# Order and waits in the odd layer of a decoder trunk: sigmoids, gate halves, decay constants and the last transposed tile

## The chip, the cores and the metric

The kernel runs on one core of one Trainium2 chip. The core has five engines with a queue each: TensorE (PE, matmuls), VectorE (DVE), ScalarE (ACT), GpSimd (POOL) and SyncE (SP, which only starts transfers here). An engine does its queue in order; between engines only semaphores set the order. The metric is the device time of one execution in microseconds.

## The reference, cut to what matters

Two residual layers over a sequence of 1024 tokens of width 1024, in float32. The first (even) layer is sparse attention beside gated linear attention; the change does not touch what it computes. The second (odd) is a Griffin recurrent block:

```python
h = rmsnorm(x, pre_norm[1])
xr, g = jnp.split(h @ odd_w_in, [1024], axis=-1)     # 1024 x 2048 weights
xr = causal_dwconv(xr, conv_w, conv_b)               # width 4
r = sigmoid(blockwise(xr, w_a) + b_a)                # 4 blocks of 256 x 256
i = sigmoid(blockwise(xr, w_x) + b_x)
a = exp(-8 * r * softplus(-lam))
u = sqrt(-expm1(2 * log_a)) * (i * xr)
hs = recurrence(a, u)                                # h_t = a_t h_(t-1) + u_t
mix = (hs * silu(g)) @ odd_w_out
x = x + rmsnorm(mix, post_norm[1])
```

## The kernel before

The order on each engine is written out by hand, engine by engine; there is no scheduler. A float32 product is made of three fp32r matmuls: each operand is split into a high part (ACT copies it to fp32r, names ending in H) and a low part (DVE or POOL subtracts, names ending in L), and PE adds high x high, high x low and low x high (three, L1583; its matmuls are L1588 to L1590). One matmul has 128 x 128 weights and 512 columns.

**Even output projection and norms (from about 675 us in the trace).** PE makes one tile of 128 tokens at a time (out_tile, 48 matmuls) and between tiles transposes the normalised tile before it into PSUM (turn_h1, L1894, 8 transposes from hn1). ACT copies the transposed tile to h1H (L1040), DVE subtracts to h1L (L1472) and adds to h1l_done. PE's next transposes wait for that semaphore, because they write the same banks. In the loop over tiles DVE does for tile t: post-norm, residual, pre-norm (L1463), and then the split of tile t-1. At t = 4 it calls odd_decay() (L1338 to L1352), 24 operations on 128 x 8 elements that make the constants of the decay; ACT needs them only before the odd layer's weights.

**Odd input projection.** 16 column chunks of weights, each in two halves of 512 tokens (odd_chunk(i), 24 matmuls, banks 0, 1, 6 and 7 in turn). Half 0 of the tokens needs tiles 0 to 3 only, so the first two chunks run before the last tile (7) is transposed; the third needs all tiles.

**The four recurrent blocks n = 0 to 3,** each of 2 x 128 channels (halves j = 0, 1). PE computes the gates (block_gates(n)): per j two groups g = 0, 1 of 12 matmuls into banks 2-3 and 4-5. A group waits, through gate_sig, until ACT's sigmoid (L1079) has emptied that bank pair. ACT writes the sigmoids to t_r and t_i, one buffer per j, shared by all blocks. Then ACT makes the decay (t_a) and a tanh, DVE the ratio, ACT the square root, and DVE multiplies (L1516) and scans (L1517, the recurrence, function recur), and multiplies the result with silu_g (L1521, function gated, which adds to y_done). silu_g comes from PSUM: ACT takes its sigmoid (silu_of, L1070), DVE multiplies it with the bank (silu_half, L1511, adds to silu_g_done), which frees the bank. sigmoids(n) in ACT's queue waits for both gated products of block n-1.

**Odd output projection.** For k = 0 to 7 (the 128-channel slices of y) PE adds to four token tiles at a time (final_part(t, k), 6 matmuls; banks 2, 4, 0, 6 and their neighbours), then tiles 4 to 7 one by one. It needs, per k, the weights w2oH / w2oL (ACT L756, POOL L606) and the split of y (split_y on ACT, low_y on DVE, L1525). Tiles 2 and 3 use banks 0-1 and 6-7, which hold the last block's silu input until silu_half has run.

Of the kernel before, what the change touches and what calls it, by code (L numbers as in the profile page):

```python
# [19 lines left out]
ALU = mybir.AluOpType  # L20
# [6 lines left out]
KD = D // P  # L27
# [10 lines left out]
LRU_BLOCKS = 4  # L38
# [43 lines left out]
def build(nc, x, rel_bias, pre_norm, post_norm, even_w_in, even_gate_w2, gate_b2, even_w_out,  # L82
# [13 lines left out]
    def sem(name):  # L96
        return ctx.enter_context(nc.semaphore(name))
# [8 lines left out]
    y = at("y", [P, KD, T], F32, R0)  # L106
# [245 lines left out]
    gw_in, gw_hi, gw_lo, gw_used = sem("gw_in"), sem("gw_hi"), sem("gw_lo"), sem("gw_used")  # L352
    xr_ready, conv_done, xch_done, xcl_done = sem("xr_ready"), sem("conv_done"), sem("xch_done"), sem("xcl_done")
    odd_full, xr_pad, sgg_done, silu_g_done = sem("odd_full"), sem("xr_pad"), sem("sgg_done"), sem("silu_g_done")
    input_gated = sem("input_gated")
    gate_full, gate_sig, decay_done, tanh_done, ratio_done, mult_done, y_done = (
        sem(n) for n in ("gate_full", "gate_sig", "decay_done", "tanh_done", "ratio_done", "mult_done", "y_done"))
    x2_in, o2_out = [sem("x2_in0"), sem("x2_in1")], [sem("o2_out0"), sem("o2_out1")]
# [384 lines left out]
    def _(act):  # L743
        def high(c):

            act.wait_ge(raw_in[c % 2], 16 * (c // 2 + 1))
            if C_WOE <= c < C_ODD or c >= C_WOO:
                k = c - (C_WOE if c < C_ODD else C_WOO)
                if c < C_ODD:
                    act.wait_ge(proj_full, len(PRODUCTS))  # L750
                    act.activation(woH[:, k, :], raw_row[:, c % 2, :], ACT.Copy).then_inc(w_hi, 1)
                else:
                    act.wait_ge(gate_full, 4 * LRU_BLOCKS)
                    if k >= 2:
                        act.wait_ge(odd_full, len(ODD_HALVES) - (2 if k == 2 else 0))
                    act.activation(w2oH[k][:, :], raw_row[:, c % 2, :], ACT.Copy).then_inc(w_hi, 1)  # L756
                return
            if c >= C_ODD:
                i = c - C_ODD
                if i == 2:  # L760
                    act.wait_ge(mix_full, NT)
                if i >= 3:
                    act.wait_ge(odd_full, ODD_HALVES.index((i - 3, 1)) + 1)
                act.activation(w_slot_H[i % 3][:, :, :], raw[:, c % 2, :, :], ACT.Copy).then_inc(w_hi, 1)  # L764
                return
            if c >= C_AV:
                act.wait_ge(proj_full, last_product(before_in_slot(c)) + 1)
            act.activation(wH[:, dst_slot(c), :, :], raw[:, c % 2, :, :], ACT.Copy).then_inc(w_hi, 1)  # L768
# [301 lines left out]
                act.activation(silu_g[:, j, hf * HALF:(hf + 1) * HALF], ps[:, ODD_BANK[i % 4], :], ACT.Sigmoid).then_inc(sgg_done, 1)  # L1070

        def sigmoids(n):
            if n:
                act.wait_ge(y_done, 2 * n)
            for j in range(2):
                for g, dst, bias in ((0, t_r, bias_a), (1, t_i, bias_x)):
                    act.wait_ge(gate_full, 4 * n + 2 * j + g + 1)
                    b = S_BANK[g]
                    act.activation(dst[:, j, :].rearrange("p (b w) -> p b w", b=2), ps[:, b:b + 2, :], ACT.Sigmoid,  # L1079
                                   bias=bias[:, 2 * n + j:2 * n + j + 1]).then_inc(gate_sig, 1)  # L1080
# [13 lines left out]
        def split_y(k):  # L1094
            if k < 2:
                act.wait_ge(conv_done, 2 * LRU_BLOCKS)
            elif k >= 6:
                act.wait_ge(input_gated, 2 * LRU_BLOCKS)
            act.wait_ge(y_done, k + 1)
            act.activation(ysH[k][:, :], y[:, k, :], ACT.Copy).then_inc(ys_hi, 1)  # L1100
# [40 lines left out]
        split_y(5)  # L1141
        silu_of(n, 1)
        high(C_WOO + 3)
        split_y(6)
        high(C_WOO + 4)
        split_y(7)
        for k in range(5, KD):
            high(C_WOO + k)

        for t in range(NT):  # L1150
# [6 lines left out]
    def _(dve):  # L1157
        steps = Tally(dve_step)

        def own(ins):  # L1160

            steps(ins)
            dve.wait_ge(dve_step, steps.n)
# [44 lines left out]
        n = 0  # L1208
# [247 lines left out]
        for t in range(NT + 1):  # L1456
            if t < NT:
                after(t, S_BANK[t % 2], wpost, post_rms, xt1, tmp1, x1_in, post_done, x1_ready)
                dve.wait_ge(rms1_ready, t + 1)
                own(dve.reciprocal(rstd[:, t:t + 1], rms[:, t:t + 1]))  # L1460
                if t >= 2:
                    dve.wait_ge(h1_turned, t - 1)
                dve.scalar_tensor_tensor(hn1[:, t % 2, :], xt1[:, t % 2, :], rstd[:, t:t + 1], wpre1[:, :],  # L1463
                                         ALU.mult, ALU.mult).then_inc(h1_ready, 1)
                if t == 4:
                    odd_decay()
            if t:
                u = t - 1
                dve.wait_ge(h1h_done, u + 1)
                toks = slice(u * P, (u + 1) * P)  # L1470
                for i in range(2):
                    ins = dve.tensor_tensor(h1L[i][:, :, toks], ps[:, 6 + i, :].rearrange("p (k n) -> p k n", n=P),  # L1472
                                            h1H[:, 4 * i:4 * i + 4, toks].bitcast(F32), ALU.subtract)
                ins.then_inc(h1l_done, 1)

        dve.wait_ge(mix_full, NT)
        dve.memset(xr[:, :, 0:3], 0.0).then_inc(xr_pad, 1)
# [35 lines left out]
        def recur(n, j):  # L1513
            dve.wait_ge(mult_done, 2 * n + j + 1)
            dve.wait_ge(input_gated, 2 * n + j + 1)
            own(dve.tensor_tensor(t_i[:, j, :], t_i[:, j, :], t_r[:, j, :], ALU.mult))  # L1516
            own(dve.tensor_tensor_scan(y[:, 2 * n + j, :], t_a[:, j, :], t_i[:, j, :], 0.0, ALU.mult, ALU.add))  # L1517

        def gated(n, j):
            dve.wait_ge(silu_g_done, 4 * n + 2 * j + 2)  # L1520
# [35 lines left out]
            silu_half(n, 0, hf)  # L1556
        low_y(3)
        recur(n, 0)
        gated(n, 0)
        recur(n, 1)  # L1560
        for k in (4, 5):
            low_y(k)
        for hf in range(2):
            silu_half(n, 1, hf)
        gated(n, 1)
        for k in (6, 7):
            low_y(k)
        dve.wait_ge(row_in, 48)

# [7 lines left out]
    def _(pe):  # L1577
# [323 lines left out]
        with rounds(pe, (NT - 2) // 2) as i:  # L1901
            for s in range(2):
                out_tile(2 * i + s + 2, s, *even, post_done, mix_full)
                turn_h1(2 * i + s + 1, 1 - s)
        def odd_chunk(i):
            c, hf = ODD_HALVES[i]
            if hf == 0:
                pe.wait_ge(w_lo, C_ODD + c + 1)
            if i >= 4:
                conv, gates = evictions(i - 4)  # L1910
                if ODD_SEQ[ODD_HALVES[i - 4][0]][1] < 2:
                    pe.wait_ge(xr_ready, conv)
                else:
                    pe.wait_ge(silu_g_done, gates)
            weights_first(ODD_BANK[i % 4], (w_slot_H[c % 3], w_slot_L[c % 3]), hf,
                          xs=(lambda k: h1H[:, k, :], lambda k: h1L[k // 4][:, k % 4, :])).then_inc(odd_full, 1)

        def block_gates(n):
            pe.wait_ge(xcl_done, 2 * n + 2)
# [11 lines left out]
                    last.then_inc(gate_full, 1)  # L1931

        odd_chunk(0)
        odd_chunk(1)
        turn_h1(NT - 1, 1)
        pe.wait_ge(post_done, NT)
        pe.wait_ge(h1h_done, NT)
        pe.wait_ge(h1l_done, NT)
# [16 lines left out]
        for k in range(KD):  # L1955
            pe.wait_ge(w_lo, C_WOO + k + 1)
            pe.wait_ge(ys_lo, k + 1)
            for t in range(4):
                if k == 0 and t >= 2:
                    pe.wait_ge(silu_g_done, 4 * LRU_BLOCKS - 2 * (3 - t))  # L1960
                last = final_part(t, k)
                if k == KD - 1:
                    last.then_inc(mix2_full, 1)
        for t in range(4, NT):
# [58 lines left out]
```

## Time and profile before

| | before |
|---|---|
| median of 3 runs | 1117.87 us (1117.31 to 1119.39) |
| the profiled execution | 1114.39 us |
| its span, first to last instruction | 1112.6 us |
| its mean granted TensorE clock | 0.961 |
| PE busy | 1011.4 us (91%) |
| DVE busy | 689.8 us (62%) |
| ACT busy | 458.0 us (41%) |
| POOL busy | 268.1 us (24%) |

How to read the rows below. A row of a timeline gives the start in us, the duration in us, engine, line, operation, output<-inputs, shape, the number of merged instructions (x), and in brackets the idle time of the engine just before and who ended it. A row of the list of waits reads: engine, what waited, its line, what it waited for and its line, then us in total, times, longest. A row on one tile's instructions gives the count, then min/median/max ns and first and last start in us. A row of busy time by stretch gives the stretch, its length, the busy us of PE, weight load, DVE, ACT and POOL (instructions), the granted clock (1.00 is 2.4 GHz, 0.50 is 1.2 GHz), DMA share and GB/s. Ends of matmuls are modelled.

### The profile page before, as it was taken

To read this page: it belongs to the slowest core of one execution; us is meant where nothing else is said; L and a number is where in the kernel's file an instruction comes from. 1 tells how busy PE (TensorE), PEld (TensorE's weight loads), DVE (VectorE), ACT (ScalarE), POOL (GpSimd) and SP (SyncE) were. 2 spreads that over 40 slices of the span, in tenths; PEclk is the share of its full clock that TensorE was granted. 3 is DMA by queue.
4 is the path that set the end of the run, shared out by engine and by line. 5 is a ranking of instruction groups with operands and counts; after the bars stand their busy time and mean duration, and the time that the engine had idled before them with its cause. 6 is when DMAs were issued, how large, how long until landed. Compare 5 with 4: busy or idle time off the path is not lost.

```text
span 1112.6 us, 14632 instructions
## 1 busy us (share of the span) xinstructions
PE 1011.4 (91%) x5642; PEld 815.4 (73%) x5642; DVE 689.8 (62%) x1220; ACT 458.0 (41%) x780; POOL 268.1 (24%) x199
## 2 busy tenths in 40 slices
PE   4996889989999999789999778989999999895997
PEld 3885679968877776557777566878788888684885
DVE  5314679997779597874554462574539393967042
ACT  6323552253422323335555563433246363573031
POOL 2210212102332322313131564120313122124000
PEclk8998999989999999899999898999999999997999
DMA  7251102101112223101010434322211121112052
GB/s 242 63 71 38 39 1 77 39 1 38 57 56 87 76 67 114 40 25 43 16 53 24 156 106 154 111 75 76 81 52 57 38 57 39 38 38 92 22 189 75
DMA packets 71738, 75.81 MB, mean 68 GB/s; under 512 B 5064, under 2 KB 58360, under 8 KB 71672
## 3 DMA queue, kind: packets, MB, share of 16 engines
q1 hardware_dynamic: 70400, 73.30, 21.1%
q10 hardware_dynamic: 1272, 1.62, 1.3%
q8 instruction: 43, 0.70, 0.3%
q14 instruction: 23, 0.19, 0.1%
HBM read 58.13 MB, written 16.25 MB: 67 GB/s over the span
## 4 chain that ended last, share of the span: by engine, by line
PE 76%; DVE 13%; ACT 5%; issue 4%; POOL 1%; DMA 1%; DVEq 0%; SPq 0%; POOLq 0%; ACTq 0%
PE ps L1588 21%; PE ps L1590 20%; PE ps L1589 20%; PE ps L1833 2%; PE ps L1817 2%; PE ps L1676 2%; PE ps L1768 1%; DVE prob L1370 1%; PE ps L1678 1%; PE ps L1765 1%; PE ps L1677 1%; ACT relu L861 1%; DVE ysL L1525 1%; PE ps L1736 1%; DVE y L1517 1%
## 5 line engine op out<-in xcount | busy, mean ns | idle before, releaser
L1588 PE MATMUL ps<-hH,wH 128*128 128x512 f32 x384 | 159.1, 414 | 15.5 <-DVE qkL L1358 10.0
L1228 DVE TENSOR_SCALAR_CACHE_REDUCE junk<-score,cand 128x384 bf16<-128x384 f32 (+2 forms) x192 | 169.7, 942 | 1.3
L1590 PE MATMUL ps<-hH,wL 128*128 128x512 f32 x384 | 152.7, 398 | 0.0
L1589 PE MATMUL ps<-hL,wH 128*128 128x512 f32 x384 | 152.3, 397 | 0.0
L612 POOL TENSOR_TENSOR wL<-raw,wH 128x1024 fp32r<-128x1024 f32 x32 | 77.1, 2413 | 157.3 <-ACT wH L768 157.3
L1588 PE MATMUL ps<-h1H,w_slot_H 128*128 128x512 f32 x256 | 100.4, 392 | 2.5 <-DVE h1L L1472 2.5
L1590 PE MATMUL ps<-h1H,w_slot_L 128*128 128x512 f32 x256 | 100.3, 392 | 0.0
L1589 PE MATMUL ps<-h1L,w_slot_H 128*128 128x512 f32 x256 | 100.2, 391 | 0.0
L1588 PEld LDWEIGHTS ps<-hH,wH 128*128 128x128 f32 x384 | 73.6, 192 | 35.3 <-issue 21.3
L1590 PEld LDWEIGHTS ps<-hH,wL 128*128 128x128 f32 x384 | 73.6, 192 | 16.2
L1589 PEld LDWEIGHTS ps<-hL,wH 128*128 128x128 f32 x384 | 73.9, 192 | 13.3
L1588 PE MATMUL ps<-wH,hH 128*128 128x256 f32 x256 | 74.7, 292 | 0.0
L1589 PE MATMUL ps<-wL,hH 128*128 128x256 f32 x256 | 73.6, 288 | 0.0
L1590 PE MATMUL ps<-wH,hL 128*128 128x256 f32 x256 | 73.6, 287 | 0.0
L609 POOL TENSOR_TENSOR w_slot_L<-raw,w_slot_H 128x1024 fp32r<-128x1024 f32 x16 | 41.3, 2582 | 132.2 <-ACT w_slot_H L764 132.2
L973 ACT ACTIVATE prob<-prob,small 128x128 f32<-128x128 f32 (+7 forms) x64 | 49.7, 777 | 46.5 <-DVE small L1376 46.4
L1446 DVE RECIPROCAL small<-small 128x1 f32<-128x1 f32 x16 | 2.6, 161 | 102.7 <-ACT small L781 102.7
L984 ACT ACTIVATE pT<-ps 128x512 f32<-128x512 f32 (+3 forms) x96 | 41.9, 487 | 57.7 <-PE ps L1817 57.5
L1370 DVE CUSTOM_DVE_ANT_0 prob<-ps,score 128x384 f32<-128x384 f32 (+5 forms) x48 | 42.7, 890 | 31.4 <-POOL score L692 24.9
L1588 PE MATMUL ps<-w2oH,ysH 128*128 128x512 f32 x128 | 50.8, 397 | 12.1 <-DVE silu_g L1511 11.7
L1588 PEld LDWEIGHTS ps<-h1H,w_slot_H 128*128 128x128 f32 x256 | 48.5, 189 | 12.8 <-issue 2.7
L1589 PEld LDWEIGHTS ps<-h1L,w_slot_H 128*128 128x128 f32 x256 | 48.5, 189 | 10.1
(242 smaller groups left out, 2266.7 us busy)
## 6 DMA issues: line engine op xcount, KB each, us to landing
raw<-in_even_w_in SPq DMA_DIRECT2D x32, 512.0 KB, 4.0
xt<-in_x SPq DMA_DIRECT2D x16, 512.0 KB, 5.6
raw<-in_odd_w_in SPq DMA_DIRECT2D x16, 512.0 KB, 3.9
gate_d<-gst SPq DMA_DIRECT2D x16, 256.0 KB, 2.2
raw_row<-in_even_w_out SPq DMA_DIRECT2D x8, 512.0 KB, 3.4
x_d<-xt SPq DMA_DIRECT2D x8, 512.0 KB, 2.6
raw_row<-in_odd_w_out SPq DMA_DIRECT2D x8, 512.0 KB, 3.2
xt<-x_d SPq DMA_DIRECT2D x8, 512.0 KB, 4.7
```

Of the source, the lines that this page charges most:

```text
L609: pool.tensor_tensor(w_slot_L[s][:, :, :], raw[:, c % 2, :, :], w_slot_H[s][:, :, :].bitcast(F32), ALU.subtract).then_inc(w_lo, 1)
L612: pool.tensor_tensor(wL[:, s, :, :], raw[:, c % 2, :, :], wH[:, s, :, :].bitcast(F32), ALU.subtract).then_inc(w_lo, 1)
L973: act.activation(prob[:, i, 0:w], prob[:, i, 0:w], ACT.Exp, bias=nmx[:, c:c + 1], accum_out=lsum[:, c:c + 1]).then_inc(exp_done[e], 1)
L984: act.activation(pT[:, e, 0:m * P], ps[:, TURN_BANK[e], 0:m * P], ACT.Copy).then_inc(turn_out, 1)
L1228: return steps(dve.tensor_scalar(junk1[:, j % 3, 0:(qb + 1) * P], score_of(qb), threshold, None, op, ALU.add, accum_out=dst[:, j:j + 1]))
L1370: dve.tensor_tensor_reduce(out=prob[:, i, 0:w].rearrange("p (b w) -> p b w", b=banks), in0=ps[:, b:b + banks, 0:wb], in1=mask_of(qb).rearr ...
L1588: pe.matmul(dst, lH, rH, start=k == 0, stop=False)
L1589: pe.matmul(dst, lH, rL, start=False, stop=False)
L1590: return pe.matmul(dst, lL, rH, start=False, stop=k == nk - 1)
L1676: yield pe.matmul(ps[:, b + i, 0:wb], qh, kh[:, cols], start=True, stop=False)
L1817: last = pe.transpose(ps[:, TURN_BANK[e], i * P:(i + 1) * P], prob[:, buffer_of(n, e), (first + i) * P:(first + i + 1) * P], ident[:, :])
L1833: both = [pe.matmul(ps[e * A_DIM:(e + 1) * A_DIM, 7, 0:P], v[:, kb, (2 * p + e) * A_DIM:(2 * p + e + 1) * A_DIM], pT[:, e, i * P:(i + 1) * ...
```

## The change

Four edits.

1. sigmoids(n) on ACT waits, per half j, for a new semaphore recurred that recur(n-1, j) adds to after its scan, instead of once for both gated products of block n-1.
2. In the last block DVE does the two silu halves of j = 1 directly behind recur(3, 0), and all of low_y(4) to low_y(7) behind the second gated product. On ACT the weights of k = 4 and k = 5 each move one place ahead. On PE tile 3 of the output projection skips k = 0 and makes it up at k = 1, and so does its wait for the silu halves.
3. odd_decay() is called behind the split of tile 3 instead of ahead of it.
4. PE transposes tile 7 between the two halves of the sum over k of odd chunk 1.

```diff
         def sigmoids(n):
-            if n:
-                act.wait_ge(y_done, 2 * n)
             for j in range(2):
+                if n:
+                    act.wait_ge(recurred, 2 * (n - 1) + j + 1)
                 for g, dst, bias in ((0, t_r, bias_a), (1, t_i, bias_x)):
...
         high(C_WOO + 3)
+        high(C_WOO + 4)
         split_y(6)
-        high(C_WOO + 4)
+        high(C_WOO + 5)
         split_y(7)
-        for k in range(5, KD):
+        for k in range(6, KD):
             high(C_WOO + k)
...
                                          ALU.mult, ALU.mult).then_inc(h1_ready, 1)
-                if t == 4:
-                    odd_decay()
             if t:
                 u = t - 1
...
                 ins.then_inc(h1l_done, 1)
+            if t == 4:
+                odd_decay()
...
-            own(dve.tensor_tensor_scan(y[:, 2 * n + j, :], t_a[:, j, :], t_i[:, j, :], 0.0, ALU.mult, ALU.add))
+            dve.tensor_tensor_scan(y[:, 2 * n + j, :], t_a[:, j, :], t_i[:, j, :], 0.0, ALU.mult, ALU.add).then_inc(recurred, 1)
+            dve.wait_ge(recurred, 2 * n + j + 1)
...
         recur(n, 0)
+        for hf in range(2):
+            silu_half(n, 1, hf)
         gated(n, 0)
         recur(n, 1)
-        for k in (4, 5):
-            low_y(k)
-        for hf in range(2):
-            silu_half(n, 1, hf)
         gated(n, 1)
-        for k in (6, 7):
+        for k in range(4, KD):
             low_y(k)
...
         odd_chunk(0)
-        odd_chunk(1)
+        odd_chunk(1, range(KD // 2))
         turn_h1(NT - 1, 1)
+        odd_chunk(1, range(KD // 2, KD))
...
             for t in range(4):
-                if k == 0 and t >= 2:
-                    pe.wait_ge(silu_g_done, 4 * LRU_BLOCKS - 2 * (3 - t))
-                last = final_part(t, k)
+                if (k, t) == (0, 2):
+                    pe.wait_ge(silu_g_done, 4 * LRU_BLOCKS - 2)
+                if (k, t) == (1, 3):
+                    pe.wait_ge(silu_g_done, 4 * LRU_BLOCKS)
+                    final_part(t, 0)
+                if (k, t) != (0, 3):
+                    last = final_part(t, k)
```

How this moves the instructions. DVE, last block, from the product ahead of the first scan to the last split of y, before (line numbers of the kernel before):

```order
L1516 TENSOR_TENSOR t_i<-t_i,t_r 128x1024
L1517 SCALAR_TENSOR_TENSOR y<-t_a,t_i 128x1024
L1521 TENSOR_TENSOR y<-y,silu_g 128x1024
L1516 TENSOR_TENSOR t_i<-t_i,t_r 128x1024
L1517 SCALAR_TENSOR_TENSOR y<-t_a,t_i 128x1024
L1525 TENSOR_TENSOR ysL_159<-y,ysH_151 128x1024
L1525 TENSOR_TENSOR ysL_160<-y,ysH_152 128x1024
L1511 TENSOR_TENSOR silu_g<-ps,silu_g 128x512 x2
L1521 TENSOR_TENSOR y<-y,silu_g 128x1024
L1525 TENSOR_TENSOR ysL_161<-y,ysH_153 128x1024
L1525 TENSOR_TENSOR ysL_162<-y,ysH_154 128x1024
```

And the same stretch now (the line numbers are one or two higher):

```order
L1517 TENSOR_TENSOR t_i<-t_i,t_r 128x1024
L1518 SCALAR_TENSOR_TENSOR y<-t_a,t_i 128x1024
L1512 TENSOR_TENSOR silu_g<-ps,silu_g 128x512 x2
L1523 TENSOR_TENSOR y<-y,silu_g 128x1024
L1517 TENSOR_TENSOR t_i<-t_i,t_r 128x1024
L1518 SCALAR_TENSOR_TENSOR y<-t_a,t_i 128x1024
L1523 TENSOR_TENSOR y<-y,silu_g 128x1024
L1527 TENSOR_TENSOR ysL_159<-y,ysH_151 128x1024
L1527 TENSOR_TENSOR ysL_160<-y,ysH_152 128x1024
L1527 TENSOR_TENSOR ysL_161<-y,ysH_153 128x1024
L1527 TENSOR_TENSOR ysL_162<-y,ysH_154 128x1024
```

The silu halves of j = 1 went from behind two splits of y, in eighth place, to third place, behind the first scan; the four splits now stand together at the end.

PE, start of the output projection (ysH_147 and ysL_155 are k = 0, ysH_148 and ysL_156 k = 1; w2oH_163 and w2oH_164 their weights), the six matmuls of tile 3 that arrive behind tile 2 of k = 1, with what they wait for:

```order
 L1590 MATMUL ps<-w2oH_164,ysL_156 128x512
+L1588 MATMUL ps<-w2oH_163,ysH_147 128x512 [waits silu_g_done]
+L1589 MATMUL ps<-w2oL_171,ysH_147 128x512
+L1590 MATMUL ps<-w2oH_163,ysL_155 128x512
+L1588 MATMUL ps<-w2oH_163,ysH_147 128x512
+L1589 MATMUL ps<-w2oL_171,ysH_147 128x512
+L1590 MATMUL ps<-w2oH_163,ysL_155 128x512
 L1588 MATMUL ps<-w2oH_164,ysH_148 128x512
```

Before, the same six stood 18 matmuls further ahead, directly behind tile 2 of k = 0, with the same wait.

PE, odd chunk 1, where the transposes of tile 7 (from hn_126) now stand:

```order
 L1589 MATMUL ps<-h1L_131,w_slot_H_134 128x512
 L1590 MATMUL ps<-h1H,w_slot_L_137 128x512
+L1894 MATMUL ps<-ident,hn_126 128x128 x8
 L1588 MATMUL ps<-h1H,w_slot_H_134 128x512
 L1589 MATMUL ps<-h1L_132,w_slot_H_134 128x512
```

They stood 12 matmuls later, between the end of chunk 1 and the start of chunk 2.

## Rows read from the trace of the kernel before

**Rows 1.** The page, part 4: the chain that ended last, by engine.

```profile
PE 76%; DVE 13%; ACT 5%; issue 4%; POOL 1%; DMA 1%; DVEq 0%; SPq 0%; POOLq 0%; ACTq 0%
```

**Rows 2.** The list of waits, engine PE, 690 to 1113 us.

```profile
PE ps L1588 <- DVE silu_g L1511: 11.7, 1, 11.7
PE ps L1588 <- ACT t_r L1079: 4.8, 1, 4.8
PE ps L1894 <- DVE h1L L1472: 3.4, 1, 3.4
PE ps L1588 <- DVE h1L L1472: 2.5, 1, 2.5
PE ps L1588 <- DVE tmp L1449: 0.3, 1, 0.3
```

**Rows 3.** The timeline of PE at tile 4 of the even output projection.

```profile
748.50 1.06 PE L1894 MATMUL ps<-ident,hn 128*128 128x128 f32 x8 [3.37 <-DVE h1L L1472]
```

**Rows 4.** The timeline of DVE beside it.

```profile
742.29 0.17 DVE L1340 TENSOR_SCALAR small<-small 128x8 f32<-128x8 f32 x1
...
747.07 1.28 DVE L1472 TENSOR_TENSOR h1L<-ps,h1H 128x512 fp32r<-128x512 f32 x2
```

**Rows 5.** The timeline of PE, odd chunks 1 and 2.

```profile
781.14 0.39 PE L1588 MATMUL ps<-h1H,w_slot_H 128*128 128x512 f32 x1
...
783.87 1.04 PE L1894 MATMUL ps<-ident,hn 128*128 128x128 f32 x8
787.43 0.47 PE L1588 MATMUL ps<-h1H,w_slot_H 128*128 128x512 f32 x1 [2.53 <-DVE h1L L1472]
...
791.84 0.39 PE L1588 MATMUL ps<-h1H,w_slot_H 128*128 128x512 f32 x1
```

**Rows 6.** The timeline of DVE beside it.

```profile
779.45 1.28 DVE L1472 TENSOR_TENSOR h1L<-ps,h1H 128x512 fp32r<-128x512 f32 x2
```

**Rows 7.** The timeline of PE, gates of block 3.

```profile
973.60 0.80 PE L1588 MATMUL ps<-xcH,gwH 128*128 128x512 f32 x1 [4.81 <-ACT t_r L1079]
...
981.72 0.39 PE L1588 MATMUL ps<-h1H,w_slot_H 128*128 128x512 f32 x1
```

**Rows 8.** The timeline of DVE beside it, end of block 2.

```profile
962.81 2.29 DVE L1517 TENSOR_TENSOR_SCAN y<-t_a,t_i 128x1024 f32<-128x1024 f32 x1
...
966.39 2.29 DVE L1517 TENSOR_TENSOR_SCAN y<-t_a,t_i 128x1024 f32<-128x1024 f32 x1
...
971.18 1.23 DVE L1521 TENSOR_TENSOR y<-y,silu_g 128x1024 f32<-128x1024 f32 x1
```

**Rows 9.** The timeline of ACT beside it.

```profile
972.44 1.11 ACT L1079 ACTIVATE t_r<-ps,small 128x1024 f32<-128x1024 f32 x1 [8.45 <-DVE y L1521]
```

**Rows 10.** The timeline of PE, start of the odd output projection.

```profile
1019.46 0.79 PE L1588 MATMUL ps<-w2oH,ysH 128*128 128x512 f32 x1 [11.74 <-DVE silu_g L1511]
...
1024.86 0.39 PE L1588 MATMUL ps<-w2oH,ysH 128*128 128x512 f32 x1
```

**Rows 11.** The timeline of ACT, DVE and POOL there, 1003.8 to 1013.0 us.

```profile
1004.18 1.09 ACT L1070 ACTIVATE silu_g<-ps 128x512 f32<-128x512 f32 x2
...
1006.29 3.02 POOL L606 TENSOR_TENSOR w2oL<-raw_row,w2oH 128x1024 fp32r<-128x1024 f32 x1 [2.54 <-ACT w2oH L756]
...
1007.20 3.19 DVE L1521 TENSOR_TENSOR y<-y,silu_g 128x1024 f32<-128x1024 f32 x1
...
1012.57 3.42 POOL L606 TENSOR_TENSOR w2oL<-raw_row,w2oH 128x1024 fp32r<-128x1024 f32 x1 [3.25 <-ACT w2oH L756]
```

**Rows 12.** The timeline of DVE further on.

```profile
1018.13 1.27 DVE L1511 TENSOR_TENSOR silu_g<-ps,silu_g 128x512 f32<-128x512 f32 x2
```

**Rows 13.** The instructions on tile silu_g, line L1511.

```profile
L1511 DVE TENSOR_TENSOR silu_g<-ps,silu_g x16: 673/678/683, 849.3 to 1018.7; 128x512 f32<-128x512 f32 x16
```

**Rows 14.** The instructions on tile w2oL, line L606.

```profile
L606 POOL TENSOR_TENSOR w2oL<-raw_row,w2oH x8: 2390/2762/3423, 989.6 to 1030.3; 128x1024 fp32r<-128x1024 f32 x8
```

**Rows 15.** Busy time by stretch, 800 to 960 us.

```profile
800.00:960.00 160.00, 160.00 (x707) 132.51 (x706) 106.87 (x77) 84.06 (x89) 39.74 (x15) 1.00 0.17 50
```

More of the change, by code:

```diff
@@ L354, in build @@
     odd_full, xr_pad, sgg_done, silu_g_done = sem("odd_full"), sem("xr_pad"), sem("sgg_done"), sem("silu_g_done")
-    input_gated = sem("input_gated")
+    input_gated, recurred = sem("input_gated"), sem("recurred")
     gate_full, gate_sig, decay_done, tanh_done, ratio_done, mult_done, y_done = (
@@ L1904, in _, with odd_chunk @@
                 turn_h1(2 * i + s + 1, 1 - s)
-        def odd_chunk(i):
+        def odd_chunk(i, ks=range(KD)):
             c, hf = ODD_HALVES[i]
-            if hf == 0:
+            if hf == 0 and ks[0] == 0:
                 pe.wait_ge(w_lo, C_ODD + c + 1)
@@ L1914, in odd_chunk @@
                     pe.wait_ge(silu_g_done, gates)
-            weights_first(ODD_BANK[i % 4], (w_slot_H[c % 3], w_slot_L[c % 3]), hf,
-                          xs=(lambda k: h1H[:, k, :], lambda k: h1L[k // 4][:, k % 4, :])).then_inc(odd_full, 1)
+            last = weights_first(ODD_BANK[i % 4], (w_slot_H[c % 3], w_slot_L[c % 3]), hf,
+                                 xs=(lambda k: h1H[:, k, :], lambda k: h1L[k // 4][:, k % 4, :]), ks=ks)
+            if ks[-1] == KD - 1:
+                last.then_inc(odd_full, 1)
         def block_gates(n):
```

## The prediction

> **What bounds the kernel now.** First the page's chain of work that ended last, to see which engine holds the end: TensorE (PE) has 76% of it, VectorE (DVE) 13%, ScalarE (ACT) 5% [rows 1]. So a microsecond is won only where PE stands still or runs below full clock. Next the list of PE's waits from 690 us on, the stretch that the edits touch. It has five entries, and the reader should see that they are single events: 11.7 us until a DVE product on silu_g, 4.8 us until the ACT sigmoid t_r, 3.4 and 2.5 us until a DVE split h1L, and 0.3 us until a DVE product on tmp [rows 2]. Nothing else holds PE there. Third, PE's timeline around each of the four large ones, for what comes behind a wait: the pitch of the matmuls. At full clock 12 of them take 783.87 - 781.14 = 2.73 us, 0.2275 us each [rows 5]; behind three of the four waits it is about twice that for a few microseconds. Last, the timelines of DVE, ACT and POOL beside each wait, for what released it and what else was queued there.
>
> The profiler draws a matmul 0.39 us long although the next starts 0.2275 us behind it, so a stall costs the idle figure plus 0.16 us.
>
> **The change part by part.** No engine gets an instruction more or fewer; only order and waits change. I take the four waits in order of time.
>
> *Decay constants behind the split (tile 4 of the norm loop).* DVE runs the 24 tiny operations of odd_decay from 742.29 until the split h1L(3) starts at 747.07, 4.78 us [rows 4]. PE's transposes of tile 4 need that split and stand from 744.97 to 748.50, 3.37 + 0.16 = 3.53 us [rows 3]. With the split first it starts at 742.3 and ends near 743.6, before PE asks. The 4.78 us then lie behind the split and end at 748.4, just where the split ended before (747.07 + 1.28), so DVE's next work, the post-norm of tile 5, starts when it did. The behind-split DVE work (hn1 of tile 5, split of tile 4) keeps its absolute time while PE comes 3.5 us sooner; from 749 on PE had no wait at all until 784.9, and one further tile is 48 x 0.2275 = 10.9 us of matmuls, so I cost this at nothing. The clock did not fall here, so the gain is **3.5 us**.
>
> *Last tile turned inside odd chunk 1.* The eight transposes of tile 7 now stand where the second half of chunk 1 began, 781.14, instead of at 783.87 [rows 5]. They need the split of tile 6, which ends at 779.45 + 1.28 = 780.73 [rows 6]: ready 0.4 us before. From the transposes' start to the matmul that their copy and split release it took 787.43 - 783.87 = 3.56 us [rows 5], so the release comes at 784.7. PE meanwhile does the transposes (0.8 us, estimated from the 1.04 us row less its drawn tail) and the 12 matmuls of 2.73 us, also until 784.7. The wait is gone. Behind it the 12 matmuls from 787.43 to 791.84 took 4.41 us instead of 2.73 [rows 5], the price of the lower clock. With both gone the position of 791.84 is reached at 784.7 + 2.73 = 787.4: **4.4 us**. Bounds: 4.4 us, and nothing if the transposes themselves wait a microsecond or more and the last split comes late again; 2.7 us if only the idle time goes. I take 4.4, since both releases are met by rows, though by tenths.
>
> *Sigmoids after each recurrence.* Block 3's first sigmoid waited for the last product of block 2: that ends at 971.18 + 1.23 = 972.41, and ACT starts at 972.44 after 8.45 us idle [rows 8, 9]. PE had done two of block 3's four gate groups and stood from 968.63 until 973.60 for the first bank [rows 7]. Now the sigmoids of half 0 need only the scan that ends at 962.81 + 2.29 = 965.10, those of half 1 the scan that ends at 968.68 [rows 8]. The first gate group is in PSUM 12 matmuls before 968.63, at 965.9, later than 965.10, so its sigmoid (1.11 us [rows 9]) ends near 967.3, and PE does not stop at 968.63. The second group's ends near 970.0, and PE asks for that bank at 971.4. From 968.63 the other 24 matmuls take 24 x 0.2275 = 5.46 us and end at 974.09 instead of 981.72 [rows 7]: **7.6 us**, of which 5.0 idle and 2.6 lower clock. In blocks 1 and 2 PE had no such wait [rows 2], so nothing comes from them. In the ACT queue the decays behind the sigmoids need all four, and move with them.
>
> *Last gate half right behind the first recurrence, PE's first tiles reordered.* In the output projection PE did tiles 0 to 2 of k = 0 and stood from 1007.56 to 1019.46 for the silu half that frees tile 3's banks [rows 10]; it stood behind two products, a scan and two splits of y in DVE's queue, at 1018.13 [rows 12]. Its input, ACT's sigmoids, was there at 1004.18 + 1.09 = 1005.3, and the first recurrence leaves DVE at 1007.20, where the gating product starts now [rows 11]. The two halves (0.68 us each, in all 16 cases [rows 13]) take that place and end near 1008.5. PE does tiles 0 to 2 of k = 1 first (18 matmuls, 4.1 us) and asks for the banks at 1011.6: 3.1 us to spare. By 1024.86 the old order had done 15 matmuls behind the wait [rows 10]; the new one is there at 1007.56 + 15 x 0.2275 = 1010.97: **13.9 us**.
>
> What is late next there? PE needs k = 2 at 1014.4 and each further k 5.5 us later: 1019.8, 1025.3, 1030.7, 1036.2, 1041.7. The weight splits on POOL of before would do as they are: k = 3 ends at 1009.3, k = 4 at 1016.0 [rows 11], k = 5 and 6 before the last one starts, and that starts at 1030.3 [rows 14]. On ACT the weights of k = 4 now stand ahead of split_y(6), and those of k = 5 ahead of split_y(7), which only brings them sooner. ysL(4) is now behind two gating products, one product and one scan: from 1008.5 on 1.23 x 4 + 2.29 = 7.2 us, until 1015.7. The DVE product at 1007.20 took 3.19 us instead of 1.23 while POOL was in an operation [rows 8, 11]; if all four products are held so, 2 us each, ysL(4) is ready at 1023.5, still 1.8 us early. So this edit costs nothing new.
>
> The Trainium skill, "SBUF — State Buffer", section "Who interferes with whom", says that a DVE instruction with two SBUF inputs is blocked whole by a GpSimd instruction that reads SBUF, and one with a single SBUF input is not. The stretched product agrees; the silu halves read one operand from PSUM and by that rule can stand beside POOL's operation at 1006.29 unharmed. If the rule were wrong they would end 2 us later, at 1010.5, still before 1011.6, so the sum is the same either way.
>
> **Sum.** 3.5 + 4.4 + 7.6 + 13.9 = 29.4 us. The profiled execution took 1114.39 us with a span of 1112.6; it becomes 1085.0, with a span of 1083.2. The median of the plain runs, 1117.87, is 3.5 us above it, and I carry the same difference: **1088.5 us**, 2.6% less.
>
> **The rivals.**
>
> *A. The turned tile gains little* (15%). Its two margins are tenths of a microsecond, and a late split of tile 6 puts the wait back. For it: of the four edits only this one has no slack. Against: all times in it move together with PE. It loses 1.7 us (the idle goes, a slow stretch stays) to 4.4: 1090.2 to 1092.9.
> The Trainium skill, "TensorE: Matmul & The Clock Gate", Part 4 (PE-mode transpose), says that transposes don't count as work for the clock gate, which speaks against putting them amid a chunk. Behind the transposes at 748.50 this trace shows no slow stretch, though they followed an idle time.
>
> *B. DVE and ACT don't follow PE in the last block* (10%). If something else (a weight, a POOL collision) held the DVE chain of block 3 at its old times, the silu halves would end at 1008.5 while PE, 7.6 us earlier, asks at 1004.0: a stall of 4.5 us and, as behind the others, some 2.5 us of slow clock. 1095.5. Against: that chain starts with the sigmoids of PE's last gates, and its queues hold nothing ahead of them that PE does not release.
>
> *C. The sigmoid's wait was not the bound* (3%): the 7.6 us stay, 1096.1. Against: 0.03 us between the product's end and the sigmoid's start [rows 8, 9].
>
> *D. More comes back than the profiled execution shows* (8%). The plain runs are 3.5 us longer than the profiled one; if that sits in longer slow stretches behind the same four stalls, it goes with them: 1085.0.
>
> *E. Slower: the clock falls in work without pause* (2%). With the stalls gone PE would have no pause but 0.3 us from 745 us to the end. If the granted clock then dropped to the 1.2 GHz level for a stretch, each 2 us of it would cost 1: from 59 us of such a stretch the 29.4 are eaten, and at 70 us the time is 1123.5. Against: from 800 to 960 us PE was 160.00 us busy out of 160 at a granted clock of 1.00, the 2.4 GHz level [rows 15].
>
> **How the numbers follow.** The forecast has 60%, A 15%, B 10%, D 8%, C 3%, E 2%, and 2% are left for what I don't see. About the forecast itself lie 2 us either way: slow stretches of other length, a split that ends a little late. The range from 1083.5 to 1094.5 holds the forecast, A and D, and leaves out B, C and E. A measurement here can tell some 0.2% from no change, 2.2 us. Every case but E and part of the unseen is faster by far more: faster 97%, the same 1%, slower 2%.
>
> **What would show it.** PE's list of waits from 690 us on should hold no entry above 1 us, and the granted clock read 1.00 from 780 to 1100. Transposes of tile 4 follow the matmul before them at once; chunk 2 starts within 0.3 us of chunk 1's end; ACT's first sigmoid of block 3 comes within 1 us of its gate group. A wait of PE on silu_g at tile 3 would show B, one on h1L behind chunk 1 would show A. I am wrong if a stall larger than 2 us appears at a place that had none, above all a wait on ysL or w2oL at k = 4 to 7, or if the four stalls are gone and the time is still above 1095.

## The result and the profile after

| | before | changed |
|---|---|---|
| median | 1117.59 us (4 runs) | 1087.27 us (4 runs) |
| lowest to highest | 1116.26 to 1119.39 | 1086.38 to 1089.96 |
| the profiled execution | 1114.39 us | 1089.96 us |
| its span | 1112.6 us | 1088.2 us |
| its granted clock | 0.961 | 0.964 |

The ratio is 0.9739, 95% interval 0.9721 to 0.9756: 30 us less, where 29.4 were forecast (1088.5 us). The profiled execution, however, fell by 24.4 us only, and its span is 5.0 us above the forecast one. That has to be explained first.

Both traces show PE's first matmul of the even output projection behind a wait of 3.45 us. Up to there no instruction is moved. The columns are start, duration, engine and line, instruction, idle before. The kernel before:

```profile
673.54 0.77 PE L1588 MATMUL ps<-woH,msH 128*128 128x512 f32 x1 [3.45 <-DVE msL L1439]
```

The changed kernel:

```profile
677.89 0.76 PE L1588 MATMUL ps<-woH,msH 128*128 128x512 f32 x1 [3.45 <-DVE msL L1440]
```

The changed kernel's profiled execution came to this point 4.35 us late. In the 14 profiled executions of this case it lies anywhere between 673.4 and 678.4 us, with the same instructions ahead of it. So spans of single executions say little about an edit of 3 us. What does say something is the distance from the first transposes (L1894, behind the first tile of that projection) to the last matmul, which I call the worked stretch below. Before it ran from 697.83 to 1104.84, 407.01 us:

```profile
697.83 1.04 PE L1894 MATMUL ps<-ident,hn 128*128 128x128 f32 x8
...
760.32 1.04 PE L1894 MATMUL ps<-ident,hn 128*128 128x128 f32 x8
...
1003.48 0.39 PE L1588 MATMUL ps<-w2oH,ysH 128*128 128x512 f32 x1
...
1104.84 0.39 PE L1590 MATMUL ps<-w2oH,ysL 128*128 128x512 f32 x1
```

Now it runs from 702.05 to 1080.41:

```profile
702.05 1.03 PE L1894 MATMUL ps<-ident,hn 128*128 128x128 f32 x8
...
1080.41 0.39 PE L1590 MATMUL ps<-w2oH,ysL 128*128 128x512 f32 x1
```

That is 378.36 us, 28.65 us less, against 29.4 forecast. The list of PE's waits from 678 us on (waits in us, times, longest) tells the rest; of the five entries of [rows 2] the four large ones are gone, and one new one has come:

```profile
PE ps L1588 <- DVE msL L1440: 3.5, 1, 3.5
PE ps L1894 <- DVE h1L L1471: 0.6, 1, 0.6
PE ps L1588 <- DVE tmp L1450: 0.3, 1, 0.3
```

The first is the wait at 677.89 above, ahead of the edits. The timeline of PE at the four places:

```profile
749.21 1.04 PE L1894 MATMUL ps<-ident,hn 128*128 128x128 f32 x8
...
761.72 1.06 PE L1894 MATMUL ps<-ident,hn 128*128 128x128 f32 x8 [0.55 <-DVE h1L L1471]
...
782.59 1.04 PE L1894 MATMUL ps<-ident,hn 128*128 128x128 f32 x8
...
786.24 0.39 PE L1588 MATMUL ps<-h1H,w_slot_H 128*128 128x512 f32 x1
...
788.99 0.39 PE L1588 MATMUL ps<-h1H,w_slot_H 128*128 128x512 f32 x1
...
971.23 0.39 PE L1588 MATMUL ps<-h1H,w_slot_H 128*128 128x512 f32 x1
...
992.99 0.39 PE L1588 MATMUL ps<-w2oH,ysH 128*128 128x512 f32 x1
```

The reader should compare each with its partner, less the offset that both traces have at that point. Transposes of tile 4: 748.50 before [rows 3], 749.21 now, where the offset had been +4.22 since 702.05: 3.5 us won. Tile 5: 760.32 before, 761.72 now, offset +1.40 instead of +0.71: 0.7 us lost. From the transposes of tile 6 on the offset is +1.45. The start of chunk 2 comes at 786.24, where 787.43 [rows 5] plus this offset would be 788.88, and the point 12 matmuls on at 788.99 instead of 791.84 + 1.45: 4.3 us won in all. The end of the gates: 981.72 [rows 7] against 971.23, an offset of -10.49 instead of -2.85: 7.6 us. The output projection starts at the same offset, 1003.48 against 992.99, and its last matmul comes at 1080.41 instead of 1104.84, an offset of -24.43 instead of -10.49: 13.9 us. The granted clock (the last but two of the columns here) is 1.00 around the three places where it had fallen to the lower level:

```profile
780.00:790.00 10.00, 10.00 (x50) 8.23 (x49) 3.48 (x6) 4.39 (x6) 2.79 (x2) 1.00 0.16 55
960.00:970.00 10.00, 10.00 (x46) 8.29 (x45) 9.86 (x8) 3.96 (x4) 0.00 (x0) 1.00 0.00 0
1000.00:1010.00 10.00, 10.00 (x46) 8.27 (x45) 9.93 (x5) 3.13 (x4) 6.62 (x2) 1.00 0.39 134
```

The 0.7 us is what the forecast lacks. DVE and POOL beside tile 5 show where it comes from. DVE:

```profile
746.52 1.28 DVE L1471 TENSOR_TENSOR h1L<-ps,h1H 128x512 fp32r<-128x512 f32 x2
747.72 0.16 DVE L1341 TENSOR_SCALAR small<-small 128x8 f32<-128x8 f32 x1
...
751.82 0.17 DVE L1350 TENSOR_SCALAR small<-small 128x8 f32<-128x8 f32 x1
752.03 2.27 DVE L1351 TENSOR_TENSOR small<-small 128x8 f32<-128x8 f32 x1
...
754.61 0.15 DVE L1447 RECIPROCAL small<-small 128x1 f32<-128x1 f32 x1
```

POOL:

```profile
751.88 2.39 POOL L725 TENSOR_TENSOR msL<-mixT,msH 128x1024 fp32r<-128x1024 f32 x1 [9.38 <-ACT msH L1019]
```

The 24 operations of the decay constants took 6.9 us instead of the 4.78 of [rows 4], because one of them, with 8 elements per partition, took 2.27 us instead of 0.17. It began 0.15 us behind POOL's subtraction msL and ended as that ended (752.03 + 2.27 = 754.30, 751.88 + 2.39 = 754.27). In the kernel before POOL's subtraction began behind the last of the 24:

```profile
747.63 2.38 POOL L725 TENSOR_TENSOR msL<-mixT,msH 128x1024 fp32r<-128x1024 f32 x1 [9.37 <-ACT msH L1019]
```

### The profile page after: what moved, and what is told of

It reads as the page before. It is cut to its first block, busy times and chain, and to the rows that moved or that the text cites. A ratio compares the mean times of both kernels' runs of the same rounds, so it can differ in the third digit from the quotient of the medians.

```text
span 1088.2 us, 14635 instructions
## 1 busy us (share of the span) xinstructions
PE 1011.9 (93%) x5642; PEld 817.2 (75%) x5642; DVE 696.0 (64%) x1220; ACT 458.8 (42%) x780; POOL 272.1 (25%) x199
## 4 chain that ended last, share of the span: by engine, by line
PE 82%; DVE 8%; ACT 5%; issue 3%; POOL 1%; DMA 1%; DVEq 0%; SPq 0%; POOLq 0%; ACTq 0%
PE ps L1588 23%; PE ps L1589 22%; PE ps L1590 22%; PE ps L1833 3%; PE ps L1817 2%; PE ps L1676 2%; DVE prob L1371 1%; PE ps L1768 1%; PE ps L1678 1%; PE ps L1765 1%; PE ps L1677 1%; ACT relu L861 1%; PE ps L1736 1%; DVE rank L1334 1%; DVE rank L1333 1%
## 5 line engine op out<-in xcount | busy, mean ns | idle before, releaser
L1218 DVE SCALAR_TENSOR_TENSOR score<-relu,wq,score 128x384 f32<-128x384 f32 (+5 forms) x42 | 42.1, 1002 | 21.5 <-ACT relu L861 18.0
L692 POOL TENSOR_TENSOR score<-nearm,near 128x256 f32<-128x256 bf16 x48 | 31.8, 675 | 96.1 <-DVE small L1371 95.6
L1590 PEld LDWEIGHTS ps<-h1H,w_slot_L 128*128 128x128 f32 x256 | 48.1, 188 | 10.0
```

What stands on the lines that cost most here:

```text
L692: pool.tensor_tensor(dst, nearm[:, qb, NEAR - w:NEAR], near[:, p % 2 * 2 + e, NEAR - w:NEAR], ALU.add).then_inc(near_ready, 1)
L1218: dve.scalar_tensor_tensor(score_of(qb), relu[:, n % 2, 0:w], wq[:, qb, h:h + 1], score_of(qb), ALU.mult, ALU.add).then_inc(acc_done, 1)
L1590: return pe.matmul(dst, lL, rH, start=False, stop=k == nk - 1)
```

## The experiments

Three theories stood at the start. (1) Each of the four edits removes its own wait, with the sizes of the forecast, and they add up. (2) Of the edit to the last gate half, the move on DVE does the work, and PE's new order adds little to it. (3) The new wait at tile 5 is POOL's subtraction holding up one small DVE operation. The rivals are told with each experiment. The table has them all; ratios are to the kernel before on the same chip.

| | median us | ratio, 95% interval | worked stretch, us | against the changed kernel |
|---|---|---|---|---|
| changed kernel | 1087.27 | 0.9739, 0.9721 to 0.9756 | 378.36 | |
| e1 decay ahead of the split | 1092.69 | 0.9774, 0.9750 to 0.9797 | 381.24 | +2.88 |
| e2 turn behind chunk 1 | 1092.38 | 0.9773, 0.9748 to 0.9799 | 382.64 | +4.28 |
| e3 sigmoids wait for products | 1096.10 | 0.9807, 0.9779 to 0.9836 | 386.14 | +7.78 |
| e4 gate half late | 1102.10 | 0.9858, 0.9831 to 0.9886 | 392.81 | +14.45 |
| e5 decay at tile 6 | 1087.79 | 0.9742, 0.9724 to 0.9759 | 377.65 | -0.71 |
| e7 DVE's move alone | 1087.58 | 0.9737, 0.9720 to 0.9754 | 379.47 | +1.11 |
| e8 PE's order alone | 1101.52 | 0.9866, 0.9845 to 0.9887 | 390.88 | +12.52 |
| e11 PE's order, old ACT order | 1098.69 | 0.9841, 0.9823 to 0.9859 | 388.88 | +10.52 |
| e12 decay at tile 6, old ACT order | 1085.54 | 0.9721, 0.9703 to 0.9740 | 377.64 | -0.72 |
| e9 fillers with two inputs | 1088.66 (1 run) | | 378.47 | +0.11 |
| e6 fillers with one input | 1085.38 (1 run) | | 377.65 | -0.71 |
| e10 fillers tensor_scalar | 1086.64 (1 run) | | 378.52 | +0.16 |

### Each edit undone by itself

**e1_decay_ahead.**

```diff
                                          ALU.mult, ALU.mult).then_inc(h1_ready, 1)
+                if t == 4:
+                    odd_decay()
...
-            if t == 4:
-                odd_decay()
```

> The changed kernel with one edit undone: odd_decay() stands again ahead of the split of tile 3. My theory: PE waits 3.4 us at the transposes of tile 4 again, and the new 0.55 us wait at the transposes of tile 5 is gone. The edit is worth 3.5 - 0.7 = 2.8 us, so this is 2.8 us slower than the changed kernel: 27.6 us faster than before, ratio to before about 0.9753. Rival (the small wait at tile 5 belongs to another edit): 3.5 us slower, and the 0.55 us wait still there.

The worked stretch is 2.88 us longer. PE waits 3.4 us at tile 4 and no longer at tile 5, as the list of its waits from 690 us on shows in full:

```profile
PE ps L1894 <- DVE h1L L1473: 3.4, 1, 3.4
PE ps L1588 <- DVE tmp L1450: 0.3, 1, 0.3
```

So the small wait belongs to this edit: the first theory holds, its rival does not.

**e2_turn_behind_chunk.**

```diff
-        odd_chunk(1, range(KD // 2))
+        odd_chunk(1)
         turn_h1(NT - 1, 1)
-        odd_chunk(1, range(KD // 2, KD))
```

> The changed kernel with the transposes of tile 7 again behind chunk 1. My theory: PE waits 2.5 us for the split h1L behind them; if the lower clock follows as in the kernel before, 4.3 us slower than the changed kernel, else 2.6 us. Rival (the wait would be gone without this edit, because the rest of the norm loop runs otherwise): no difference.

4.28 us longer. The wait of 2.53 us is back, and with it the pitch of 0.43 us (here between the starts of the second and third row), as PE's timeline shows:

```profile
784.78 0.76 PE L1588 MATMUL ps<-h1H,w_slot_H 128*128 128x512 f32 x1 [2.53 <-DVE h1L L1471]
785.34 0.63 PE L1589 MATMUL ps<-h1L,w_slot_H 128*128 128x512 f32 x1
785.76 0.63 PE L1590 MATMUL ps<-h1H,w_slot_L 128*128 128x512 f32 x1
```

**e3_sigmoids_wait_products.**

```diff
         def sigmoids(n):
+            if n:
+                act.wait_ge(y_done, 2 * n)
             for j in range(2):
-                if n:
-                    act.wait_ge(recurred, 2 * (n - 1) + j + 1)
```

> The changed kernel with ACT's sigmoids waiting again for both gated products of the block before. My theory: PE waits 4.8 us in the gates of block 3 and runs about 12 matmuls at the 1.2 GHz level behind it: 7.6 us slower than the changed kernel, about 22.8 us faster than before. Rival (the output projection has slack that takes up a late gate): under 5 us slower.

7.78 us longer, with the wait of before (4.81 us there) and 12 matmuls at the lower level:

```profile
966.43 0.80 PE L1588 MATMUL ps<-xcH,gwH 128*128 128x512 f32 x1 [4.80 <-ACT t_r L1079]
```

The slow part costs 2.74 us instead of 2.66, which is about half of the 0.2 us above the forecast; the rest is not traced. The output projection has no slack that takes any of it up.

**e4_gate_half_late.**

```diff
         recur(n, 0)
-        for hf in range(2):
-            silu_half(n, 1, hf)
         gated(n, 0)
         recur(n, 1)
+        for k in (4, 5):
+            low_y(k)
+        for hf in range(2):
+            silu_half(n, 1, hf)
         gated(n, 1)
-        for k in range(4, KD):
+        for k in (6, 7):
             low_y(k)
...
-                if (k, t) == (0, 2):
-                    pe.wait_ge(silu_g_done, 4 * LRU_BLOCKS - 2)
-                if (k, t) == (1, 3):
-                    pe.wait_ge(silu_g_done, 4 * LRU_BLOCKS)
-                    final_part(t, 0)
-                if (k, t) != (0, 3):
-                    last = final_part(t, k)
+                if k == 0 and t >= 2:
+                    pe.wait_ge(silu_g_done, 4 * LRU_BLOCKS - 2 * (3 - t))
+                last = final_part(t, k)
```

and the two weight copies on ACT back in their places.

> The changed kernel with the last gate half again behind two splits of y on DVE, tile 3 at k = 0 on PE and the old places of two weight copies on ACT. My theory: PE waits 11.7 us on silu_g and has a slow stretch behind: 13.9 us slower than the changed kernel, 16.5 us faster than before. Rival (the DVE chain gained less than PE from the other edits, so the wait would be longer): 15 us or more slower.

14.45 us longer, with the same idle time as before, to the hundredth:

```profile
1009.70 0.80 PE L1589 MATMUL ps<-w2oH,ysH 128*128 128x512 f32 x1 [11.74 <-DVE silu_g L1511]
```

Behind it 12 matmuls ran slow where it had been 9 in the kernel before, at 0.2 us each; that makes the 0.5 us above 13.9. The four differences add to 29.39 us, the whole to 28.65: the edits are independent but for these tenths.

### What the gate half's edit consists of

**e7_dve_move_alone.**

```diff
-                if (k, t) == (0, 2):
-                    pe.wait_ge(silu_g_done, 4 * LRU_BLOCKS - 2)
-                if (k, t) == (1, 3):
-                    pe.wait_ge(silu_g_done, 4 * LRU_BLOCKS)
-                    final_part(t, 0)
-                if (k, t) != (0, 3):
-                    last = final_part(t, k)
+                if k == 0 and t >= 2:
+                    pe.wait_ge(silu_g_done, 4 * LRU_BLOCKS - 2 * (3 - t))
+                last = final_part(t, k)
```

> The changed kernel, but PE again asks for tile 3's banks at k = 0; DVE keeps the silu halves behind the first recurrence. My theory: in the trace of the changed kernel the halves end at 998.0 and PE has done tiles 0 to 2 of k = 0 at 997.07, so PE waits 0.9 us and the clock stays: 0.9 us slower than the changed kernel, not to be told in the times. Rival (PE's new order carries the edit): 5 us slower or more, a wait of several us on silu_g.

PE waits, and its clock stays up:

```profile
997.96 0.50 PE L1588 MATMUL ps<-w2oH,ysH 128*128 128x512 f32 x1 [0.82 <-DVE silu_g L1512]
```

1.11 us in the stretch; the times can't tell it from the changed kernel. So 12.8 of the 13.9 us come with DVE's move (and the new places of the copies on ACT) alone; PE's new order adds the last 1.1.

**e8_pe_reorder_alone.**

```diff
         recur(n, 0)
-        for hf in range(2):
-            silu_half(n, 1, hf)
         gated(n, 0)
         recur(n, 1)
+        for k in (4, 5):
+            low_y(k)
+        for hf in range(2):
+            silu_half(n, 1, hf)
         gated(n, 1)
-        for k in range(4, KD):
+        for k in (6, 7):
             low_y(k)
```

> The changed kernel, but DVE makes the last silu halves again behind two splits of y; PE keeps tile 3 for k = 1. My theory: PE asks 4.1 us later than in the kernel before and the halves come as late as there, so it waits 11.7 - 4.1 = 7.7 us, with a slow stretch of 2 us behind: 9.7 us slower than the changed kernel. Rival (PE's new order carries the edit): under 2 us slower.

Against the rival this is plain: without DVE's move PE's order leaves the time near e4's. But the size is wrong, 12.5 us instead of 9.7. Of the 2.8 us between them 2.2 are the wait, 9.89 us instead of 7.7, and the rest is the slow stretch behind it, 2.5 us instead of 2. DVE, behind the first scan of block 3, shows a second product held up:

```profile
995.06 3.25 DVE L1523 TENSOR_TENSOR y<-y,silu_g 128x1024 f32<-128x1024 f32 x1
998.23 3.40 DVE L1517 TENSOR_TENSOR t_i<-t_i,t_r 128x1024 f32<-128x1024 f32 x1
```

and POOL two splits back to back where the kernel before had one of 3.02 us [rows 11]:

```profile
994.15 6.38 POOL L606 TENSOR_TENSOR w2oL<-raw_row,w2oH 128x1024 fp32r<-128x1024 f32 x2 [2.54 <-ACT w2oH L756]
```

The new theory was that the weight copy of k = 4, which the change puts one place ahead on ACT, brings POOL's split forward into that product.

**e11_pe_reorder_old_act.** As e8, and

```diff
         high(C_WOO + 3)
-        high(C_WOO + 4)
         split_y(6)
-        high(C_WOO + 5)
+        high(C_WOO + 4)
         split_y(7)
-        for k in range(6, KD):
+        for k in range(5, KD):
```

> PE's new order without DVE's move, as in e8, but ACT's copies of the weights of k = 4 and k = 5 in their old places too. In e8 PE waited 9.9 us instead of the 7.7 expected; a DVE product beside POOL took 3.40 us there and 1.21 in the kernel before. Theory (the earlier copy on ACT brought POOL's split of k = 4 forward into that product): with the old places the product takes 1.2 us, POOL's two splits come apart again, and PE waits 7.7 us. Rival (PE's own order, or chance): the wait stays 9.9 us.

The wait is 7.68 us and DVE's product takes 1.21:

```profile
996.16 1.21 DVE L1516 TENSOR_TENSOR t_i<-t_i,t_r 128x1024 f32<-128x1024 f32 x1
```

So the earlier copies on ACT cost DVE 2.2 us here. The stretch is 3.9 us shorter than e4's (388.88 against 392.81), which differs by PE's order alone: without DVE's move that order is worth 3.9 us, beside it only the 1.1 of e7. The two parts overlap, and their shares don't add. In the changed kernel, too, that product takes 3.42 us (at 999.87), but it stands behind the silu halves, and nothing waits for it soon.

### The small new wait

**e5_decay_tile6.**

```diff
-            if t == 4:
+            if t == 6:
                 odd_decay()
```

> The changed kernel with odd_decay() behind the split of tile 5 instead of the split of tile 3, where POOL has nothing left to do until the odd layer. My theory: the 24 operations take 4.9 us there instead of 6.9, the post-norm of tile 5 starts some 3.5 us sooner, and PE's 0.55 us wait at the transposes of tile 5 is gone: 0.7 us faster than the changed kernel, less than the times can tell, to be read in the trace. Rival (any 24 operations between a split and a post-norm make PE wait): the wait comes again at a later tile.

0.71 us shorter, and PE's only wait behind the first is the 0.3 us one. The 24 operations take 4.90 us here (766.84 to 771.74), with POOL idle. The ratio is the changed kernel's. The post-norm of tile 5 starts at once behind ACT's root, but its residual addition is now held up by POOL (2.96 us), which costs PE nothing.

**e9_two_inputs_beside_pool.** The last five operations of odd_decay() become odd_decay_end() at t = 6; in their place

```diff
+            for _ in range(5):
+                own(dve.tensor_tensor(lam_z, lam_z, lam_z, ALU.max))
```

> In the changed kernel one operation of odd_decay(), 128 x 8 with two inputs, took 2.27 us instead of 0.17 beside POOL's msL subtraction. Here the last five operations of odd_decay() move behind the split of tile 5 and five fillers with two inputs (a maximum of lam_z with itself, which changes nothing) stand in their place, so the count is the same. Theory (POOL's operation holds up a DVE operation with two SBUF inputs): one filler takes some 2.2 us. Rival (it was that line, or its data): all fillers take 0.17 us.

**e6_one_input_beside_pool.** The same with

```diff
+                own(dve.reciprocal(lam_n, lam_z))
```

> The same with five fillers of one input (a reciprocal of lam_z into lam_n, which is written anew later). Theory (two SBUF inputs are what is held up): no filler takes more than 0.25 us, the post-norm of tile 5 starts 2 us sooner than in the changed kernel and PE does not wait at the transposes of tile 5. Rival (any DVE operation is held up while POOL works): one filler takes some 2.2 us, PE waits 0.5 us.

**e10_scalar_op_beside_pool.** The same with

```diff
+                own(dve.tensor_scalar(lam_p, lam_p, 1.0, None, ALU.mult))
```

> The same with five fillers tensor_scalar on 128 x 8, one input (a product with 1.0). In the kernel before a tensor_scalar of 128 x 1024 took 2.79 us instead of 0.82 beside POOL. Theory a (an operation that reads with both ports is held up, whatever its size): one filler takes some 2.2 us. Theory b (for so few elements it reads with one port): all take 0.17 us.

The five fillers of each kernel as one merged row of DVE's timeline, e9, e6 and e10 in this order:

```profile
750.22 3.07 DVE L1350 TENSOR_TENSOR small<-small 128x8 f32<-128x8 f32 x5
```

```profile
747.74 1.16 DVE L1350 RECIPROCAL small<-small 128x8 f32<-128x8 f32 x5
```

```profile
748.13 3.11 DVE L1350 TENSOR_SCALAR small<-small 128x8 f32<-128x8 f32 x5
```

POOL's subtraction of 2.4 us starts within each: at 750.48, 748.00 and 748.41. Five operations free of it take about 1.0 us (0.2 each); reciprocals are a little longer also where POOL is idle (0.20 us instead of 0.17), and five of them, 0.23 us apart, make the 1.16. With two inputs the five take 2.1 us more than that, and so they do with tensor_scalar, though that has one input and 8 elements: the outcome that theory a of e10 gives, while the ports themselves are not to be seen in a trace. The reciprocals with one input don't wait. PE waits 0.7 us in e9 and e10 and not in e6, whose stretch is 377.65 us as in e5. So POOL's subtraction is what held the small operation up, and with it PE at tile 5: the third theory is shown. Its reason in e9 and e6, that two SBUF inputs are what is held up, is too narrow: tensor_scalar has one and waits too.

### A version from these

**e12_decay_tile6_old_act.** odd_decay() at t == 6 and the two weight copies on ACT in their old places; the rest as changed.

> The changed kernel with odd_decay() behind the split of tile 5, as in e5, and the two weight copies on ACT in their old places. Theory (the silu halves stand ahead of all that POOL can hold up, and PE needs the weights of k = 4 only 5 us later than they come): no wait of PE beyond 0.3 us, the same time as e5 and the changed kernel within 0.1%, and the DVE product behind the first gating product at 1.2 to 2 us instead of 3.4. Rival (the copies must come sooner, else PE waits for w2oL at k = 4): a wait of 1 us or more on w2oL, slower than the changed kernel.

No wait beyond the 0.3 us, stretch 377.64 us, and the product behind the first gating product takes 1.21 us. The weights of k = 4 come in time without the new places. Its ratio of 0.9721 (0.9703 to 0.9740) overlaps the changed kernel's: by the trace 0.7 us better, by the times not to be told apart.

## Why the prediction was right, point by point

**The sum.** Forecast and measured, edit by edit in the changed kernel's trace: decay constants 3.5 and 3.5; turned tile 4.4 and 4.3; sigmoids 7.6 and 7.6; gate half 13.9 and 13.9. Undone one by one they measure 2.9, 4.3, 7.8 and 14.5. These 3.5 us are what PE wins at tile 4; 0.7 go again at tile 5. The sum of 29.4 was right to 3%: 28.65 in the stretch, 30.3 between the medians.

**The step that failed** is "I cost this at nothing" for the DVE work behind the moved decay constants. Its premise, that the 4.78 us would end where the split had ended, was false: they took 6.9 us, through one collision with POOL that the trace of before foretells. The prediction puts the 24 operations between 743.6 and 748.4 us, and POOL's subtraction starts there at 747.63; the prediction weighed such collisions for the large products only. Post-norm and pre-norm of tile 5 and the split of tile 4 all came 2 us late, which ate the 1.5 us that PE's earlier arrival had left and 0.55 us more: a term of 0.7 us (the idle time and 0.16) where the sum has none.

**The turned tile's tenths.** The forecast had both releases at 784.7 in the time of before; now PE takes chunk 2 without any idle time, at 784.79 in the time of before. Rival A did not come about, and the clock stayed at 1.00 behind the transposes amid the chunk. The Trainium skill, "TensorE: Matmul & The Clock Gate", Part 4, says that transposes don't count as work for the clock in the same way as matmuls; 0.8 us of them with matmuls on both sides did nothing to it here.

**The order within the gate half.** The margin of 3.1 us that PE's new order was to give was there (PE asked at 1001.2, the halves ended at 998.0), but most of it is not needed, as e7 shows. What is late next (k = 4 to 7) was also right: of the four operations of DVE that the prediction adds up for ysL(4), the three products were held up (2.05, 3.42 and 3.24 us), the split was not, and PE still waited for none of it.

**Rivals B, C and E** did not come about; the block-3 chain moved with PE by the full 7.6 us, and PE was busy without pause but for 0.3 us from 762 us to its last matmul at a granted clock of 1.00. **Rival D** is partly what the medians show: they differ by 30.3 us, the stretch by 28.65. The 1.7 us between them is within the scatter of the first 678 us, and no run here says whether longer slow parts in the plain runs went with the waits.

**From one execution to the median.** The forecast of 1083.2 us for the span of a single execution was empty: the point where the edits begin moves by 5 us from one execution to another. Taking the profiled execution's difference to the median over, 3.5 us, is the same as taking the sum off the median. That is right only if the scatter lies ahead of the edits, which the prediction couldn't know from one trace; that it came out within 1.2 us of the measured median was in part luck.

## What to carry to other kernels

A wait of the bounding engine is priced at its idle time plus what the clock loses behind it; here that was 1.7 to 2.7 us behind eight waits of 2.5 to 11.7 us, and nothing behind the two of 3.4 us and those under 1 us. When an operation is moved on DVE, look at what POOL does at its new place, even if it is of 0.17 us: if the operation is of a kind that POOL holds up, the price is the rest of POOL's operation. And measure small edits between two marks in the trace, behind the part that scatters.

## What was not expected of the hardware

A tensor_scalar of 128 x 8 with one SBUF input waits for POOL's subtraction as one with two inputs does (3.11 and 3.07 us for five), a reciprocal of the same size does not (1.16). The Trainium skill, "SBUF — State Buffer", "Who interferes with whom", has tensor_scalar among the operations that can take the shared ports; the trace agrees, and adds that eight elements are enough. The prediction told the rule of that section as if one SBUF input were always enough to be free of POOL; for tensor_scalar e10 shows that it is not.

The hold-up goes the other way too. POOL's weight split takes 2.39 us undisturbed and 4.41 in the changed kernel, where it begins 0.07 us behind the start of DVE's scan:

```profile
1003.33 2.29 DVE L1518 TENSOR_TENSOR_SCAN y<-t_a,t_i 128x1024 f32<-128x1024 f32 x1
```

```profile
1003.40 4.41 POOL L606 TENSOR_TENSOR w2oL<-raw_row,w2oH 128x1024 fp32r<-128x1024 f32 x1 [1.19 <-ACT w2oH L756]
```

In e12 it begins 1.01 us behind the start of the scan and takes 3.47 us: each time it is longer by about what is left of the scan, which keeps its 2.29 us. In e3 POOL began first, by 0.02 us; there its split took 2.39 us and the scan 4.52:

```profile
1006.74 4.52 DVE L1518 TENSOR_TENSOR_SCAN y<-t_a,t_i 128x1024 f32<-128x1024 f32 x1
```

So of these two whichever has begun holds up the other.

The clock is less regular than the waits. The wait of 2.53 us behind the transposes of tile 7 was followed by the 1.2 GHz level both times (before, e2), the one of 3.37 to 3.39 us ahead of the transposes of tile 4 by none both times (before, e1). Why the longer one is free is open. Nor does the fall come at the same point: in the kernel before the granted clock was still 1.00 for the first half microsecond behind the wait of 2.53 us, in e2 it was 0.50 at once. Behind the wait on silu_g it was 9 slow matmuls in the kernel before, about 12 in e4, e8 and e11.
